# Output products of two finished mixers, moved into the middle of the last mixer's products

## The reference

```python
hdn = rmsnorm(x, ns[2])
mix, st_new = token_mixers(hdn, pos, p, st, chunk)   # below
x = x + rmsnorm(mix, ns[3])
...
out_ret = head_rmsnorm(flat(ro), p['ret_norm']) * jax.nn.silu(rg)
out_ssm = rmsnorm(flat(y) * jax.nn.silu(z), p['ssm_norm'])
out_gdn = head_rmsnorm(flat(go), p['gdn_norm']) * jax.nn.silu(gg)
hout = num / jnp.maximum(jnp.abs(den), jnp.exp(-m_t))[..., None]
out_ml = jax.nn.sigmoid(mo) * head_rmsnorm(flat(mh), p['mlstm_norm'])
mixed = jnp.concatenate([out_ret, out_ssm, out_gdn, out_ml], axis=-1) @ p['w_out']
```

## Time and profile before

| | us |
|---|---|
| median of 3 runs | 1483.66 |
| lowest and highest of the 3 | 1474.27, 1489.93 |
| the profiled execution | 1486.53 |
| its span from the first to the last instruction | 1484.7 |
| PE busy with matmuls | 1405.7 (95%) |
| VectorE busy | 840.6 (57%) |
| ScalarE busy | 581.9 (39%) |
| GpSimd busy | 108.6 (7%) |
| mean granted TensorE clock | 0.940 |

### The profile page before, as it was taken

One profiled execution on the slowest core, in us unless ns is written; L12 is line 12 of the kernel. 1 busy time (PEld: TensorE's weight loads), 2 busy tenths in 40 slices (PEclk: granted clock), 3 DMA queues, 4 the chain that ended last, 5 costly groups with the idle time before them and its releaser, 6 DMA issues.

```text
span 1484.7 us, 28320 instructions
## 1 busy us (share of the span) xinstructions
PE 1405.7 (95%) x11576; PEld 1341.2 (90%) x11576; DVE 840.6 (57%) x1265; ACT 581.9 (39%) x837; POOL 108.6 (7%) x157
## 2 busy tenths in 40 slices
PE   5999998999999988999989999989999998999996
PEld 4999998999976988999989999989998788999995
DVE  4455546756435774554575554576573468455454
ACT  4333344553223442333453333446323325333342
POOL 5400000000020026000000000000000200300000
PEclk9999999999976889999999999999998868999998
DMA  7855444432311339554445554434222213854450
GB/s 210 175 169 170 163 156 135 131 121 92 101 33 32 94 113 186 169 162 160 133 143 170 170 166 159 157 114 142 86 91 82 44 35 102 172 171 159 153 171 32
DMA packets 205947, 193.85 MB, mean 131 GB/s; under 512 B 29380, under 2 KB 203924, under 8 KB 205728
## 3 DMA queue, kind: packets, MB, share of 16 engines
q1 hardware_dynamic: 200432, 184.50, 40.9%
q0 software_dynamic: 4496, 6.09, 2.8%
q10 hardware_dynamic: 928, 1.95, 0.4%
HBM read 186.32 MB, written 6.19 MB: 130 GB/s over the span
## 4 chain that ended last, share of the span: by engine, by line
PE 88%; DMA 5%; DVE 4%; ACT 2%; issue 1%; SPq 1%; ACTq 0%; DVEq 0%
PE ps L619 86%; DMA ring<-in_ffn_w_up 4%; PE ps L622 2%; DVE ring_r L1910 1%; DMA big<-in_x_prompt 1%; SPq L575 1%; DVE x L1978 1%; DVE y L1919 1%; ACT whigh_r L1468 1%; DVE y L1977 0%; DMA arena<-in_state_ret 0%; ACT lnr L1492 0%; ACT r2row L1493 0%; ACT hdn L1484 0%; ACT L1488 0%
## 5 line engine op out<-in xcount | busy, mean ns | idle before, releaser
L1910 DVE TENSOR_TENSOR ring_r<-ring,whigh_r 128x2048 fp32r<-128x2048 f32 (+1 forms) x166 | 371.5, 2239 | 357.3 <-ACT whigh_r L1468 357.2
L1468 ACT ACTIVATE whigh_r<-ring 128x2048 fp32r<-128x2048 f32 (+1 forms) x166 | 310.6, 1871 | 368.4 <-PE ps L619 335.4
L619 PE MATMUL ps<-hdn,ring_r 128*128 128x288 f32 x2016 | 333.8, 299 | 0.0
L619 PE MATMUL ps<-hdn,whigh_r 128*128 128x288 f32 x1888 | 304.8, 303 | 12.3 <-DVE ring_r L1910 12.3
L619 PEld LDWEIGHTS ps<-hdn,ring_r 128*128 128x128 f32 x2016 | 296.3, 193 | 0.3
L619 PEld LDWEIGHTS ps<-hdn,whigh_r 128*128 128x128 f32 x1888 | 270.7, 192 | 15.0 <-issue 13.4
L619 PE MATMUL ps<-y_r,whigh_r 128*128 128x288 f32 x1792 | 275.2, 297 | 0.0
L619 PEld LDWEIGHTS ps<-y_r,whigh_r 128*128 128x128 f32 x1792 | 252.1, 189 | 0.0
L619 PE MATMUL ps<-big_r,whigh_r 128*128 128x288 f32 x800 | 125.4, 298 | 0.0
L619 PEld LDWEIGHTS ps<-big_r,whigh_r 128*128 128x128 f32 x800 | 112.2, 188 | 0.7
L619 PE MATMUL ps<-arena_r,whigh_r 128*128 128x288 f32 x704 | 109.4, 296 | 0.0
(11 more groups left out here) (426 smaller groups left out, 1362.3 us busy)
## 6 DMA issues: line engine op xcount, KB each, us to landing
ring<-in_ffn_w_gate SPq DMA_DIRECT2D x44, 1024.0 KB, 5.3
ring<-in_ffn_w_up SPq DMA_DIRECT2D x44, 1024.0 KB, 5.4
ring<-in_ffn_w_down SPq DMA_DIRECT2D x32, 1024.0 KB, 5.0
ring<-in_w_in SPq DMA_DIRECT2D x30, 1024.0 KB, 5.2
ring<-in_ffn_w_down SPq DMA_DIRECT2D x16, 768.0 KB, 4.3
ring<-in_w_out SPq DMA_DIRECT2D x8, 1024.0 KB, 5.0
cst<-in_const POOLq DMA_DIRECT2D x1, 1953.5 KB, 10.2
big<-in_x_prompt ACTq DMA_DIRECT2D x2, 512.0 KB, 9.0
```

What stands on the lines that cost most here:

```text
L619: return pe.matmul(out, lhsT, rhs, start=start, stop=stop, **k)
L1468: A(high(pos)[:, 0:rows * 256], ring[:, s, 0:rows * 256], ACT.Copy)\
L1910: return TT(out, in_, high, ALU.subtract)
```

## The change

On PE, in each of the two layers, the retention and gated delta parts of output tiles 0 and 1 are done between `weights_sum(0, 7)` and `out("ml", 1, 4)`. The waits that they need (`slot_ready`, `out_root` of SSD, `qx_ready` of mLSTM) move with them. Behind the mLSTM's sums only the SSD parts and the mLSTM parts remain. No other engine's list is changed.

```diff
                 after("sadd_read", "ssd")
                 weights_sum(0, 7)
+                slot_ready(l, POS_OUT)
+                after("out_root", "ssd")
+                out_part(l, 0, ("ret", "gdn"))
+                after("qx_ready", "ml")
+                out_part(l, 1, ("ret", "gdn"))
                 out("ml", 1, 4)
                 weights_sum(1, 6)
                 after("probs_ready", "ml", 2)
...
                 hold(sem("floor_ready"), l * 3 + 1)
                 weights_sum(2, 7)
-                slot_ready(l, POS_OUT)
-                after("out_root", "ssd")
-                after("qx_ready", "ml")
-                out_part(l, 0, ("ret",))
                 after("raw_made", "ml", 1)
                 after("state_last", "ml")
                 sample_add("ml")
                 after("raw_made", "ml", 2)
                 sums("ml", (1, 7))
-                out_part(l, 0, ("gdn", "ssd"))
-                out_part(l, 1, ("ret", "gdn", "ssd"))
+                for t in range(2):
+                    out_part(l, t, ("ssd",))
                 for t in range(2):
                     out_part(l, t, ("ml",)).then_inc(sem("post_product_done"), 1)
```

## The result

| | us |
|---|---|
| median of 7 runs of the changed kernel | 1492.83 |
| lowest and highest of the 7 | 1489.59, 1496.62 |
| median of 7 runs of the kernel before, same chip | 1483.45 |
| ratio, with its 95% interval | 1.0064, 1.0035 to 1.0094 |
| span of the profiled execution, before and after | 1484.7, 1494.8 |

What follows compares the result with a forecast made beforehand. PE was taken to bound the kernel (88% of the span); 2.90 - 0.30 - 0.54 = +2.06 us in layer 0 and +2.05 in layer 1, together +4.1 us, put the 1483.66 us median at 1487.8; range 1477 to 1496.

Steps and rivals of the forecast that it cites:

- The chain's delay: ScalarE and VectorE work from the second product's floors on: forecast 2.90 us later in layer 0, 2.65 in layer 1.
- the block: The 24 retention and gated delta matmuls moved on PE: forecast 5.07 us, with the clock rising 4.2 us into them.
- the rival that hides the block: The 24 matmuls fill room on PE in the middle stretch and lift the clock: 1477.6 us; chance 0.10.
- the one where the clock stays down: The clock never rises in the 24 moved matmuls and the middle stretch: +10.7 us, 1494.4 us; chance 0.18.
- the one with a high clock up to the norm: The clock stays up until the mLSTM norm, so its sums start earlier and halve: 1485.0 us; chance 0.10.
- the middle stretch: `out("ml", 1)` and `weights_sum(1)` on PE, behind the moved matmuls: forecast 3.54 us at the high clock instead of 6.13.
- The wait at the new place: PE's wait for the weights' lower half from VectorE before the moved matmuls: +0.42 us in layer 0, +0.17 in layer 1.
- `sample_add`: Six retention matmuls behind the third product: forecast to start 0.30 us earlier, waiting only for the second raw tile.
- The mLSTM part: Twelve matmuls ending the stage: forecast to start when their operand is there, -0.54 us in layer 0, -0.30 in layer 1.
- new but not a loss: PE's wait of about a microsecond behind the thinned cover, ahead of the mLSTM part; forecast to cost nothing.

Runs made afterwards that it cites:

- the block behind the event: The changed kernel with the 24 moved matmuls one step later, behind `weights_sum(1)`; 1483.36 us, 1.0006 of the kernel before.
- the delayed chain: The kernel before, PE untouched, with ScalarE making the second output weights' upper half two more times ahead of the raw tile's divisions; 1487.6 us, 1.0029.
- the freed chain: The changed kernel with ScalarE making the second output weights' upper half ahead of the second product's floors; 1482.32 us, 0.9993.
- The filled wait: The changed kernel with 16 unread matmuls of 224 columns added ahead of the mLSTM part; 1497.51 us, 1.0101.
- waits at the block's start: The changed kernel with the other three waits of the 24 moved matmuls put ahead of the wait for the weights; one run, 1489.04 us.

## Why the prediction was right in kind and less than half in size

**The chain's delay.** Right as a mechanism: the chain starts later by the block's net time, and the block behind the event, the delayed chain and the freed chain all show it. Neither the rival that hides the block holds (it cost its full 5.60 us) nor the one where the clock stays down (it rose), nor the one with a high clock up to the norm (0.50 from 485.80 to 499.00). That the result lies in the range is partly luck: the upper end was set by the case of the clock that stays down, which did not happen.

The Trainium skill, Trainium Kernel Development and Optimization, Performance Expectations, names weight-load busy time, not matmul busy time, as a good metric for how close a kernel is to its roofline. The hidden block took it as a measure of how full PE is; as such the trace doesn't bear it out in the middle stretch: weight loads were busy for 3.27 of 6.13 us, and there was no room for the block.

**The wait at the new place** was forecast at +0.42 / +0.17 and is 473.71 - 471.78 - 1.15 = +0.78 and 1197.41 - 1195.54 - 1.15 = +0.72. The term that was mis-sized is the 0.15 us between VectorE's end and PE's start: here three more waits stand behind the late one, and it is 0.60 us.

**The block** was forecast at 5.07 us and is 5.60 / 5.56, mainly since the clock rose 5.1 / 5.0 us into it and not 4.2. **The middle stretch** was forecast at 3.54 us and is 3.57.

**`sample_add`** was to win 0.30 us and won nothing. The prediction took its start before, 486.09, as the end of the six retention matmuls. It lies 0.45 us behind the raw tile at 485.64; after the change it lies 493.77 - 493.31 = 0.46 us behind it, with no matmuls in between. It had been held by the raw tile already. This is the same mis-sized term once more: the list of PE shows three waits ahead of `sample_add`, the raw tile's first, and 0.14 us with two further waits at 0.15 make 0.44. No run put these waits in another order. The forecast wait of "a few microseconds" is there, 3.49.

**The mLSTM part** came nearer to the sums by 0.55 / 0.30 us, as forecast (0.54 / 0.30): it waits for its operand and for nothing else. It starts 0.14 us behind its split. The wait is 1.97 us, not one.

**The step that was missing** is what this wait does to the clock. The sum treated it as "new but not a loss". The clock fell 0.6 us behind it, eight or nine of the twelve matmuls took 0.24 us and the transposes 1.66 instead of 1.01 us: 4.93 - 3.28 = 1.65 us in layer 0, 5.06 - 3.42 = 1.64 in layer 1. The filled wait gives back 1.58 / 1.56 of it. It is the largest single miss.

Together, in layer 0: 0.36 for the wait, 0.53 for the block, 0.03 for the middle stretch, 0.30 for `sample_add`, 1.65 for the clock, 2.87 us; the forecast was +2.06 and the result +4.93.

## What to carry to other kernels

Before you move work on the bound engine to an earlier place, look for the next event behind that place from which another engine's chain starts: work ahead of the event delays the chain by its net time, while the same work behind it can stand in the time that the chain needs anyway, as far as it doesn't delay the next such event. The work taken away from its old place was cover: cost the wait that it leaves, and the clock behind that wait as well. Look on the other engines for instructions that don't need the event but stand queued behind one that does. And where an engine waits for several things in a row, put the wait that is fulfilled last at the end.

## What the runs showed of the hardware

- Behind the start of an unbroken row of 288-column matmuls the clock rose after 4.2 us in the kernel before, after 5.1 and 5.0 us in the changed kernel, and after 2.9 us (475.17 to 478.1) and 6.0 us in the two layers of the kernel with the block behind the event. One such time, read at one place, doesn't hold for another.
- The clock fell in the mLSTM part behind waits of 1.97 and 1.99 us (changed kernel), 2.08 us (freed chain), 1.98 and 1.89 us (waits at the block's start), and did not fall behind 1.50 us (block behind the event, layer 0) nor 0.31 us (filled). Other work ahead of the waits differs too, so this shows no limit, only that a wait of about 2 us on PE can cost half the speed of what stands behind it.
- On PE a matmul behind several semaphore waits, of which the first is the late one, started 0.59 to 0.61 us behind the late engine's end with four waits (the block in the changed kernel, the freed chain and the filled one), 0.45 to 0.46 us with three (`sample_add`, before and after), 0.29 to 0.31 us with two (the third block of weights, whole products) and 0.14 us with one (the mLSTM part) or with the late one put last. The difference is about 0.15 us for each fulfilled wait behind the late one, the increment that follows a wait in this kernel included. Only the case of four was tested by an edit.
